# The first layer's attention mask, two levels earlier in POOL's chain of table instructions

## The chip, the cores and the metric

The kernel runs on one core of a Trainium2 chip. The metric is the device time of one execution in microseconds (us). Before the change three runs took 1725.45, 1729.42 and 1731.07 us; the median is 1729.42 us. The engines are called as in the profile: PE (TensorE, matmuls), DVE (VectorE), ACT (ScalarE), POOL (GpSimd) and SP (SyncE, which issues the weight transfers).

## The reference

Two layers of a transformer-like trunk over 256 tokens of width 1024. Each layer mixes tokens by three branches, and then has a feed-forward part: dense in the first layer, eight experts with the two best per token in the second. Two of the branches matter here.

```
# stick-breaking attention, 8 heads of 64, query blocks of 128
z = q @ k.T * scale
valid = key_pos < q_pos
log_stay = where(valid, log_sigmoid(-z), 0)
tail = reverse_cumsum(log_stay) - log_stay
w = where(valid, exp(log_sigmoid(z) + tail), 0)
out = w @ v
# S5 state space branch, 16 groups of 64 states
s_t = (mag * (cos(angle) + i sin(angle))) * s_{t-1} + b_t     # complex
y = c_re . s_re - c_im . s_im
# merged = g0 * (attention @ w_a) + g1 * (ssm @ w_b) + g2 * (conv @ w_c)
```

## The kernel before

Activations are kept transposed (features on partitions, 256 tokens along the row), weights come as units of 1 MB through a ring of seven slots. Every weight unit is split into a high and a low part: ACT copies the high part (L1010), DVE subtracts to get the low part (L1245, 2048 elements per partition, the longest instruction that DVE has), and PE makes three products with them (L627). Each engine runs a program of its own, in order, and the engines meet only at semaphores. The order of the mixer's steps is one list for all engines, `STEPS`: q, k, v, then `z` 0 (scores of the first four heads), `bbT`, u, `softplus` 0, h, b, c, `tail` 0, `gC` 0, `bu` 0, `gC` 1, `attend` 0, `bu` 1, `gC` 2, `z` 1 and so on. Each engine leaves out the steps in which it has no part.

The attention of four heads goes: PE computes scores (`z`, L690 and L692), ACT takes Abs, Exp and Ln of them (L1080 to L1083), DVE adds the positive part (`softplus`, L1339, which signals `stay_ready`), POOL sets the invalid entries to zero (the first mask, two instructions at L1644, which signals `stay_masked`), PE adds the cumulative sums (`tail`, L698 and L700), ACT takes Exp (L1087, signals `w_ready`), POOL masks again (L1644, signals `w_masked`), PE multiplies by v (`attend`, L711 and L713).

The state space branch needs tables of cosine and sine of the angle times 0 to 255. POOL builds them in `ssm_parameters` by doubling: a level of n columns makes columns n to 2n from columns 0 to n in six instructions (L1698 to L1703) over 8 times n elements per partition, and five small ones (L1709 to L1713) square the power for the next level. There are eight levels, n from 1 to 128. After the last one `tables_ready` lets DVE rotate and scan the states (`bu`, L1366 to L1375), and POOL rotates them back (L1726 to L1731). `ssm_parameters(0)` stands ahead of all of POOL's steps of layer 0, so POOL would come to the first mask only behind the whole chain; for that reason the chain itself contains that one mask, between two levels (L1692 and L1693), and the step `softplus` 0 of layer 0 is left out of POOL's list. The second mask (step `tail` 0) stands in POOL's list behind the chain. In layer 1 the chain runs long before its tables are needed, and its masks stand in the list.

`WB` is 3: PE writes its products into three work banks in turn, and waits for the reader of the bank that it takes.

Of the kernel before, what the change touches and what calls it, by code (L numbers as in the profile page):

```python
# [7 lines left out]
def trunk_kernel(nc, x, gain_mix, w_in, lam_re, lam_im, log_dt, b_re, b_im, c_re, c_im, ssm_d, w_glu,  # L8
# [17 lines left out]
    L = x.shape[0]  # L26
# [30 lines left out]
    def rows(w):  # L57
        return w.rearrange("(k p) n -> p k n", p=P)
# [137 lines left out]
    with ctx:  # L196
# [1418 lines left out]
        def _(pool):  # L1615
            chain = [0]

            def link(ins):

                chain[0] += 1  # L1620
                ins.then_inc(pool_chain, 1)
                pool.wait_ge(pool_chain, chain[0])
# [16 lines left out]
            def mask(ready, number, masked):  # L1639

                pool.wait_ge(ready, number)
                for lo in (0, L):
                    blk = attn[:, :, lo:lo + P]
                    last = nc.gpsimd.affine_select(out=blk, in_=blk, compare_op=ALU.is_gt, fill=0.0,  # L1644
                                                   base=0, pattern=[[0, HB], [1, P]],
                                                   channel_multiplier=-1)
                    if lo == 0:
                        link(last)
                last.then_inc(masked, 1)

            def ssm_parameters(l):

                if l:
                    pool.wait_ge(states_used, l * SJ)
                    pool.wait_ge(work_done, Group((l - 1, "glu", 0)).done)
                js = slice(l * SJ, l * SJ + SJ)
                for c, (b_src, c_src) in enumerate(((b_re, c_re), (b_im, c_im))):
                    pool.dma_start(braw[:, c, :, :], b_src[l].rearrange("g p h -> (g p) h")
                                   .rearrange("(j s) h -> s j h", s=P)).then_inc(ssm_loaded, 16)
                    pool.dma_start(craw[:, c, :, :], c_src[l].rearrange("g p h -> (g p) h")  # L1660
                                   .rearrange("(j s) h -> s j h", s=P)).then_inc(ssm_loaded, 16)
                pool.dma_start(wglu[:, :, :], rows(w_glu[l])).then_inc(glu_loaded, 16)
                link(nc.gpsimd.memset(bbp[:, :, :], 0.0))
                link(nc.gpsimd.memset(cblk[:, :, :, :], 0.0))
                pool.wait_ge(ssm_loaded, 64 * (l + 1))
                pool.wait_ge(f_ready, 1)
                fr = f_re[:, js].unsqueeze(2).to_broadcast([P, SJ, GH])
                fi = f_im[:, js].unsqueeze(2).to_broadcast([P, SJ, GH])
                m = [rtmp[:, q, 0:SJ * GH].rearrange("p (j h) -> p j h", h=GH) for q in range(4)]
                link(tt(m[0], braw[:, 0, :, :], fr, ALU.mult))  # L1670
                link(tt(m[1], braw[:, 1, :, :], fi, ALU.mult))
                link(tt(m[2], braw[:, 1, :, :], fr, ALU.mult))
                link(tt(m[3], braw[:, 0, :, :], fi, ALU.mult))
                for par in range(2):
                    r = slice(par * P // 2, par * P // 2 + P // 2)
                    hs = slice(par * GH, par * GH + GH)
                    for c, op in ((0, ALU.subtract), (1, ALU.add)):
                        dst = bbp[r, c, :].rearrange("p (j h) -> p j h", h=2 * GH)[:, :, hs]
                        link(tt(dst, m[2 * c][r], m[2 * c + 1][r], op))
                    link(ts(cblk[r, 0, :, hs], craw[r, 0, :, :], 1.0, None, ALU.mult))  # L1680
                    link(ts(cblk[r, 1, :, hs], craw[r, 1, :, :], -1.0, None, ALU.mult))
                nc.gpsimd.memset(cosT[:, :, 0:1], 1.0).then_inc(bbp_ready, 1)

                pc, ps, p2, p3, p4 = [power[:, q, :] for q in range(5)]
                link(nc.gpsimd.memset(sinT[:, :, 0:1], 0.0))
                link(nc.gpsimd.tensor_copy(pc, cos1[:, js]))
                nc.gpsimd.tensor_copy(ps, sin1[:, js]).then_inc(c_ready, 1)
                pool.wait_ge(c_ready, l + 1)
                pool.wait_ge(bbp_ready, l + 1)
                n = 1  # L1690
                while n < L:
                    if l == 0 and 2 * n == L:  # L1692
                        mask(stay_ready, 1, stay_masked)  # L1693
                    old, new = slice(0, n), slice(n, 2 * n)
                    bc = pc.unsqueeze(2).to_broadcast([P, SJ, n])
                    bs = ps.unsqueeze(2).to_broadcast([P, SJ, n])
                    tmp = rtmp[:, :, :].rearrange("p t n -> p (t n)")[:, 0:SJ * n].rearrange("p (j n) -> p j n", n=n)
                    tt(cosT[:, :, new], cosT[:, :, old], bc, ALU.mult)  # L1698
                    link(tt(tmp, sinT[:, :, old], bs, ALU.mult))
                    tt(sinT[:, :, new], sinT[:, :, old], bc, ALU.mult)  # L1700
                    link(tt(cosT[:, :, new], cosT[:, :, new], tmp, ALU.subtract))
                    link(tt(tmp, cosT[:, :, old], bs, ALU.mult))
                    last = tt(sinT[:, :, new], sinT[:, :, new], tmp, ALU.add)  # L1703
                    n *= 2
                    if n == L:
                        last.then_inc(tables_ready, 1)
                        break
                    link(last)
                    link(tt(p2, pc, pc, ALU.mult))  # L1709
                    link(tt(p3, ps, ps, ALU.mult))  # L1710
                    link(tt(p4, pc, ps, ALU.mult))
                    link(tt(pc, p2, p3, ALU.subtract))
                    link(tt(ps, p4, p4, ALU.add))  # L1713

            for l in range(DEPTH):
                ssm_parameters(l)
                for kind, t in STEPS:
                    if kind == "softplus":
                        if (l, t) != (0, 0):
                            mask(stay_ready, 2 * l + t + 1, stay_masked)  # L1720
                    elif kind == "tail":
                        mask(w_ready, 2 * l + t + 1, w_masked)
                    elif kind == "bu":
                        pool.wait_ge(scanned, 2 * (l * SJ + t + 1))
                        s_re, s_im = sring[:, t % 4, 0, :], sring[:, t % 4, 1, :]
                        tt(rtmp[:, 0, :], s_re, cosT[:, t, :], ALU.mult)  # L1726
                        tt(rtmp[:, 1, :], s_im, sinT[:, t, :], ALU.mult)
                        tt(rtmp[:, 2, :], s_re, sinT[:, t, :], ALU.mult)
                        link(tt(rtmp[:, 3, :], s_im, cosT[:, t, :], ALU.mult))
                        link(tt(s_re, rtmp[:, 0, :], rtmp[:, 1, :], ALU.subtract))  # L1730
                        tt(s_im, rtmp[:, 2, :], rtmp[:, 3, :], ALU.add).then_inc(states_ready, 1)  # L1731
                        pool.wait_ge(states_ready, l * SJ + t + 1)
# [45 lines left out]
```

## Time and profile before

| | |
|---|---|
| median of three runs | 1729.42 us (1725.45 to 1731.07) |
| span of the profiled execution | 1727.6 us |
| what lies around the span, median less span | 1.8 us |
| PE busy | 1655.4 us, 96% |
| POOL busy | 252.5 us, 15% |
| DVE busy | 552.4 us, 32% |
| share of PE in the chain that ended last | 88% |
| share of POOL in it | 4% |

The profiled execution has no time of its own beside its span; the span stands 1.8 us below the median and within the three runs. "Busy" says how long an engine had an instruction in it. The chain that ended last follows the execution back from its last instruction, at each step to what released it, so its shares say which engine's speed the end hung on. The granted clock (PEclk) is a share of 2.4 GHz: 1.00 is 2.4 GHz, 0.50 is 1.2 GHz.

### The profile page before, as it was taken

To read this page: it belongs to the slowest core of one execution; us is meant where nothing else is said; L and a number is where in the kernel's file an instruction comes from. 1 tells how busy PE (TensorE), PEld (TensorE's weight loads), DVE (VectorE), ACT (ScalarE), POOL (GpSimd) and SP (SyncE) were. 2 spreads that over 40 slices of the span, in tenths; PEclk is the share of its full clock that TensorE was granted. 3 is DMA by queue.
4 is the path that set the end of the run, shared out by engine and by line. 5 is a ranking of instruction groups with operands and counts; after the bars stand their busy time and mean duration, and the time that the engine had idled before them with its cause. 6 is when DMAs were issued, how large, how long until landed. Compare 5 with 4: busy or idle time off the path is not lost.

```text
span 1727.6 us, 32135 instructions
## 1 busy us (share of the span) xinstructions
PE 1655.4 (96%) x14514; PEld 1004.5 (58%) x14514; DVE 552.4 (32%) x836; ACT 410.2 (24%) x524; POOL 252.5 (15%) x338
## 2 busy tenths in 40 slices
PE   7889989999989999899999999999999999999996
PEld 6868989999989879853332333433333323334333
DVE  6557567444454675431010011110010100111102
ACT  5442344444454523310010010100010100101002
POOL 3877278000000461000000000000000000000000
PEclk9989999999999999989999999999999999999998
DMA  9702574555545324569989999989999989999980
GB/s 279 247 25 74 153 225 148 195 179 187 179 139 172 122 74 149 218 270 358 399 324 362 397 362 383 360 341 388 391 357 398 349 336 400 358 384 377 351 332 25
DMA packets 192649, 465.12 MB, mean 269 GB/s; under 512 B 9600, under 2 KB 91520, under 8 KB 192512
## 3 DMA queue, kind: packets, MB, share of 16 engines
q1 hardware_dynamic: 189600, 461.40, 72.3%
q8 instruction: 115, 1.88, 0.4%
q0 software_dynamic: 416, 1.05, 0.3%
q10 hardware_dynamic: 2496, 0.61, 0.2%
q14 instruction: 22, 0.18, 0.0%
HBM read 461.98 MB, written 1.05 MB: 268 GB/s over the span
## 4 chain that ended last, share of the span: by engine, by line
PE 88%; POOL 4%; DVE 4%; ACT 2%; issue 1%; ACTq 0%; DVEq 0%; POOLq 0%
PE work L627 28%; PE acc L892 23%; PE acc L920 17%; PE ssm_y L892 11%; PE acc L627 5%; PE work L903 1%; PE ssm_y L737 1%; PE work L728 1%; DVE arena L1532 1%; PE work L641 1%; POOL arena L1700 1%; DVE arena L1263 1%; PE acc L698 0%; DVE parts L1245 0%; POOL arena L1703 0%
## 5 line engine op out<-in xcount | busy, mean ns | idle before, releaser
L627 PE MATMUL work<-xs,parts 128*128 128x256 f32 x3648 | 463.4, 287 | 16.8 <-DVE xs L1252 13.6
L627 PEld LDWEIGHTS work<-xs,parts 128*128 128x128 f32 x3648 | 450.1, 194 | 28.1 <-issue 25.0
L892 PE MATMUL acc<-ring,arena 128*32 128x512 f32 (+1 forms) x4096 | 435.2, 543 | 0.7 <-issue 0.7
L920 PE MATMUL acc<-ring,arena 128*32 128x512 f32 x2688 | 294.4, 592 | 1.4 <-ACT arena L1176 1.4
L1245 DVE TENSOR_TENSOR parts<-ring,parts 128x2048 fp32r<-128x2048 f32 x94 | 222.8, 2375 | 177.6 <-ACT parts L1010 177.5
L892 PEld LDWEIGHTS acc<-ring,arena 128*32 128x32 f32 x4096 | 131.0, 110 | 247.8 <-issue 227.2
L892 PE MATMUL ssm_y<-ring,arena 128*32 128x512 f32 (+1 forms) x2048 | 239.3, 539 | 0.0
L1010 ACT ACTIVATE parts<-ring 128x2048 fp32r<-128x2048 f32 x94 | 179.1, 1910 | 122.6 <-PE work L627 69.5
L920 PEld LDWEIGHTS acc<-ring,arena 128*32 128x32 f32 x2688 | 85.8, 110 | 196.6 <-issue 192.9
L1541 DVE TENSOR_TENSOR arena<-arena,acc 64x256 f32<-64x256 f32 (+1 forms) x32 | 12.5, 390 | 561.2 <-ACT arena L1171 561.2
L1171 ACT ACTIVATE arena<-acc 64x512 f32<-64x512 f32 (+1 forms) x96 | 51.6, 538 | 556.6 <-PE ssm_y L892 555.0
L892 PEld LDWEIGHTS ssm_y<-ring,arena 128*32 128x32 f32 x2048 | 66.5, 110 | 126.3 <-issue 115.3
L627 PE MATMUL acc<-hs,parts 128*128 128x256 f32 x672 | 82.8, 283 | 0.0
L627 PEld LDWEIGHTS acc<-hs,parts 128*128 128x128 f32 x672 | 81.6, 192 | 0.0
L1548 DVE COPY arena<-work 128x256 f32<-128x256 f32 (+1 forms) x32 | 12.4, 389 | 200.7 <-PE work L903 200.7
L1176 ACT ACTIVATE arena<-work 128x512 f32<-128x512 f32 (+1 forms) x32 | 17.4, 544 | 247.7 <-PE work L903 247.7
L1644 POOL TENSOR_SCALAR_AFFINE_SELECT arena<-arena 128x512 f32<-128x512 f32 x16 | 14.8, 924 | 282.8 <-DVE arena L1339 271.5
L1102 ACT ACTIVATE sig<-work 128x256 f32<-128x256 f32 x48 | 18.4, 384 | 136.7 <-PE work L627 136.7
L903 PEld LDWEIGHTS work<-ident,arena 128*128 128x128 f32 x168 | 18.3, 144 | 32.7 <-issue 23.9
L1389 DVE TENSOR_TENSOR arena<-sig,work 128x256 f32<-128x256 f32 x48 | 19.9, 415 | 53.8 <-ACT sig L1102 53.8
L903 PE MATMUL work<-ident,arena 128*128 128x128 f32 x168 | 28.2, 294 | 6.8 <-DVE arena L1532 4.4
L1726 POOL TENSOR_TENSOR arena<-arena 128x256 f32<-128x256 f32 x16 | 27.1, 1693 | 40.1 <-DVE arena L1375 40.1
(244 smaller groups left out, 1098.2 us busy)
## 6 DMA issues: line engine op xcount, KB each, us to landing
ring<-in_moe_w_gate SPq DMA_DIRECT2D x112, 1024.0 KB, 7.2
ring<-in_moe_w_up SPq DMA_DIRECT2D x112, 1024.0 KB, 9.4
ring<-in_moe_w_down SPq DMA_DIRECT2D x112, 1024.0 KB, 8.7
ring<-in_w_in SPq DMA_DIRECT2D x44, 1024.0 KB, 6.7
ring<-in_dense_w_gate SPq DMA_DIRECT2D x14, 1024.0 KB, 5.0
ring<-in_dense_w_up SPq DMA_DIRECT2D x14, 1024.0 KB, 5.0
ring<-in_dense_w_down SPq DMA_DIRECT2D x14, 1024.0 KB, 4.9
ring<-in_w_out SPq DMA_DIRECT2D x8, 1024.0 KB, 12.0
```

What stands on the lines that cost most here:

```text
L627: last = nc.tensor.matmul(out_ap, a, b, start=start and n == 0, stop=stop and n == len(pairs) - 1, skip_group_check=shared)
L641: last = nc.tensor.matmul(bank[:, 0:L], neg_ones[:, :], xnT[:, k, :], start=k == 0, stop=k == KT - 1)
L892: last = nc.tensor.matmul(region(x, ns), xe[:, k, c:c + GRP], w[:, kk, half * ns:half * ns + ns], start=k == 0, stop=k == KT - 1)
L903: last = nc.tensor.transpose(bank[:, f * P:f * P + P], erow[:, tile, f * P:f * P + P], ident[:, :])
L920: last = nc.tensor.matmul(acc[GRP * q:GRP * q + GRP, b, :], eh[:, kt % tiles, c:c + GRP], w[:, kk, half * OUT_COLS:half * OUT_COLS + OUT_C ...
L1010: nc.scalar.activation(parts[:, s % PARTS, 0, :], ring[:, n % RING, :], ACT.Copy)\
L1102: nc.scalar.activation(sig[:, n % 2, :], bank[:, 0:L], ACT.Sigmoid).then_inc(sig_ready, 1)
L1171: nc.scalar.activation(dst, src, ACT.Silu).then_inc(silu_set, 1)
L1176: nc.scalar.activation(eh[:, 0:tiles, P // 2:2 * SLOTS], bank[:, 0:tiles * P].rearrange("p (f n) -> p f n", n=P), ACT.Copy)\
L1245: tt(parts[:, s % PARTS, 1, :], ring[:, n % RING, :], parts[:, s % PARTS, 0, :].bitcast(F32), ALU.subtract).then_inc(lo_ready, 1)
L1389: tt(dst, sig[:, n % 2, :], bank[:, L:2 * L], ALU.mult).then_inc(gate_used, 1)
L1726: tt(rtmp[:, 0, :], s_re, cosT[:, t, :], ALU.mult)
```

## The change

The test that places the first layer's first mask in the chain of levels is changed from the last level (n = 128) to the one of 32 columns. Nothing else is changed.

```diff
--- before.py
+++ after.py
@@ -1689,7 +1689,7 @@
                 pool.wait_ge(bbp_ready, l + 1)
                 n = 1
                 while n < L:
-                    if l == 0 and 2 * n == L:
+                    if l == 0 and 8 * n == L:
                         mask(stay_ready, 1, stay_masked)
                     old, new = slice(0, n), slice(n, 2 * n)
                     bc = pc.unsqueeze(2).to_broadcast([P, SJ, n])
```

Of the instruction order only POOL's differs; PE, DVE, ACT and SP have the same rows in the same order. The first place is POOL ahead of the level of 32 columns (8x32 is 256 elements; L1712 and L1713 belong to the level ahead of it):

```order
 L1712 TENSOR_TENSOR power<-power 128x8
 L1713 TENSOR_TENSOR power<-power 128x8
+L1644 AFFINE_SELECT arena<-arena 128x4x128 x2
 L1698 TENSOR_TENSOR arena<-arena,power 128x8x32
 L1699 TENSOR_TENSOR arena<-arena,power 128x256
```

The mask's two instructions are added here, with their wait for `stay_ready`. The second place is POOL ahead of the level of 128 columns:

```order
 L1712 TENSOR_TENSOR power<-power 128x8
 L1713 TENSOR_TENSOR power<-power 128x8
-L1644 AFFINE_SELECT arena<-arena 128x4x128 x2
 L1698 TENSOR_TENSOR arena<-arena,power 128x8x128
 L1699 TENSOR_TENSOR arena<-arena,power 128x1024
```

They are taken out here. Behind the last level POOL's order is the same before and after: the rows are the end of the last level, the second mask, and the first rotation of states.

```order
L1701 TENSOR_TENSOR arena<-arena 128x8x128
L1702 TENSOR_TENSOR arena<-arena,power 128x1024
L1703 TENSOR_TENSOR arena<-arena 128x8x128
L1644 AFFINE_SELECT arena<-arena 128x4x128 x2
L1726 TENSOR_TENSOR arena<-arena 128x256
```

PE's order, the same before and after, has behind the tail step (L698, L700) two tiles of gate C with the state input between them, and then the attend step (L711, L713):

```order
L698 MATMUL acc<-arena,neg_incl 128x384
L700 MATMUL acc<-arena,neg_ones 128x128
L627 MATMUL work<-xs,parts 128x256 x24
L627 MATMUL work<-arena,br_slot 128x256 x2
L728 MATMUL work<-arena,bbT 128x256 x2
L627 MATMUL work<-xs,parts 128x256 x24
L627 MATMUL work<-arena,br_slot 128x256 x2
L711 MATMUL acc<-arena 64x256
```

Nothing moved on PE: the first mask releases L698 and the second one L711.

## Rows read from the trace of the kernel before

**Rows 1.** The page's head: span of the profiled execution.

```profile
span 1727.6 us, 32135 instructions
```

**Rows 2.** PE's waits, whole span: us in total, times, longest.

```profile
PE acc L698 <- POOL arena L1644: 13.4, 3, 10.6
```

**Rows 3.** PE in order of time: start, us, instruction, count, idle before.

```profile
58.73 23.27 PE L627 MATMUL work<-xs,parts 128*128 128x256 f32 x192
92.55 1.65 PE L698 MATMUL acc<-arena,neg_incl 128*128 128x384 f32 x2 [10.55 <-POOL arena L1644]
...
98.84 3.11 PE L627 MATMUL work<-xs,parts 128*128 128x256 f32 x24
...
106.78 1.03 PE L627 MATMUL work<-arena,br_slot 128*128 128x256 f32 x4
108.31 0.66 PE L711 MATMUL acc<-arena 128*64 128x256 f32 x4 [0.50 <-POOL arena L1644]
...
114.80 0.71 PE L690 MATMUL acc<-arena 64*128 64x256 f32 x4
```

**Rows 4.** POOL in order of time, 70 to 108 us.

```profile
70.44 0.62 POOL L1698 TENSOR_TENSOR arena<-arena,power 128x256 f32<-128x256 f32 x1
...
71.71 2.54 POOL L1700 TENSOR_TENSOR arena<-arena,power 128x256 f32<-128x256 f32 x1
74.22 2.78 POOL L1701 TENSOR_TENSOR arena<-arena 128x256 f32<-128x256 f32 x1
77.08 0.62 POOL L1702 TENSOR_TENSOR arena<-arena,power 128x256 f32<-128x256 f32 x1
77.78 0.73 POOL L1703 TENSOR_TENSOR arena<-arena 128x256 f32<-128x256 f32 x1
...
81.97 1.04 POOL L1698 TENSOR_TENSOR arena<-arena,power 128x512 f32<-128x512 f32 x1
...
91.15 1.34 POOL L1644 TENSOR_SCALAR_AFFINE_SELECT arena<-arena 128x512 f32<-128x512 f32 x2
92.46 1.90 POOL L1698 TENSOR_TENSOR arena<-arena,power 128x1024 f32<-128x1024 f32 x1
...
98.14 2.39 POOL L1701 TENSOR_TENSOR arena<-arena 128x1024 f32<-128x1024 f32 x1
...
102.59 4.37 POOL L1703 TENSOR_TENSOR arena<-arena 128x1024 f32<-128x1024 f32 x1
106.91 1.34 POOL L1644 TENSOR_SCALAR_AFFINE_SELECT arena<-arena 128x512 f32<-128x512 f32 x2
```

**Rows 5.** DVE in order of time, 69 to 105 us.

```profile
69.70 1.74 DVE L1339 SCALAR_TENSOR_TENSOR arena<-acc,arena 128x1536 f32<-128x1536 f32 x1
71.36 5.04 DVE L1245 TENSOR_TENSOR parts<-ring,parts 128x2048 fp32r<-128x2048 f32 x2
...
89.49 0.69 DVE L1357 TENSOR_TENSOR arena<-arena 128x512 f32<-128x512 f32 x1
102.41 2.29 DVE L1245 TENSOR_TENSOR parts<-ring,parts 128x2048 fp32r<-128x2048 f32 x1 [12.23 <-ACT parts L1010]
```

**Rows 6.** POOL in order of time, the second layer's first mask.

```profile
562.23 5.26 POOL L1644 TENSOR_SCALAR_AFFINE_SELECT arena<-arena 128x512 f32<-128x512 f32 x2 [263.43 <-DVE arena L1339]
```

**Rows 7.** Windows: stretch, length, busy (count) by engine, PEclk, DMA share, GB/s.

```profile
84.50:85.00 0.50, 0.00 (x0) 0.00 (x0) 0.50 (x1) 0.00 (x0) 0.50 (x1) 0.62 1.08 383
...
92.50:98.00 5.50, 5.45 (x13) 3.63 (x14) 0.00 (x0) 0.00 (x0) 5.42 (x3) 0.50 0.00 0
98.00:98.50 0.50, 0.50 (x3) 0.29 (x2) 0.00 (x0) 0.00 (x0) 0.50 (x2) 0.73 0.00 0
...
226.00:228.40 2.40, 0.20 (x2) 0.08 (x1) 1.63 (x4) 2.21 (x8) 2.08 (x5) 1.00 1.10 348
```

**Rows 8.** PE in order of time, the second layer's tail step.

```profile
572.84 0.81 PE L698 MATMUL acc<-arena,neg_incl 128*128 128x384 f32 x2
...
576.23 0.36 PE L627 MATMUL work<-xs,parts 128*128 128x256 f32 x1
```

## The prediction

> **What bounds the kernel now.** I read the page's busy table first: PE is busy for 96% of a span of 1727.6 us [rows 1], so a change that removes no PE work can only change PE's waits or its clock. Next the table of PE's waits: PE waits for POOL's mask ahead of the tail matmuls three times, 13.4 us in all, and one wait of 10.6 us is most of it [rows 2]. That is the wait at which this change aims. Then PE and POOL in order of time around it. PE is done with its projections at 82.00 (58.73 + 23.27), sits idle for 10.55 us and starts the tail at 92.55, when POOL's first mask is through [rows 3, 4]. It then works without a gap to 107.81, and its attend step starts at 108.31 after only 0.50 us of waiting for POOL's second mask [rows 3].
>
> The reader should see in POOL's rows that POOL never rests from 70.44 to the end of the second mask at 108.25 (106.91 + 1.34), and that this mask comes behind the last level of the tables (102.59 + 4.37 = 106.96) [rows 4]. So the attend step is released by the length of POOL's whole chain, not by the place of the first mask in it. The 10.55 us idle of PE are real, but they are slack of a race that POOL loses a moment later: PE has 0.50 us to spare at 108.31. PE's order keeps attend in front of everything that follows, so PE can't run past it.
>
> **The change part by part.**
>
> *The early mask's wait.* At 70.44 POOL begins the level of 32 columns. In the changed order it first waits for DVE's softplus, which starts at 69.70 and ends at 71.44 [rows 4, 5]. POOL starts the mask about 0.06 us later, at 71.50, so 1.06 us of POOL's time are lost. Before, the result was 19.7 us old when the mask came, and nothing was waited for. Queued behind this wait are all of levels 32, 64 and 128, the second mask and the rotations: DVE waits for the tables, PE for the second mask.
>
> *The mask itself.* Two instructions leave 91.15 to 92.46 (1.31 us of pitch) and come in at 71.50. As far as they run alone they cost nothing net. But at 71.36 DVE starts two weight splits in a row, 5.04 us together, until 76.40 [rows 5]. POOL's instructions that fall on such a split are long: L1700 takes 2.54 and L1701 2.78 us there, and the same sizes on L1702 and L1703, a moment later, 0.62 and 0.73 us [rows 4]. That is 1.92 + 2.05 = 3.97 us of blocking. The second layer has just the new situation, the mask directly behind the softplus: its two instructions take 5.26 us there instead of 1.34 [rows 6, 4], 3.92 us of blocking. So the mask takes over the blocking from L1700 and L1701, one for the other: 3.92 - 3.97 = -0.05 us. The mask ends at 71.50 + 5.26 = 76.76, and nobody is late for it, since PE comes to the tail at 82.00.
>
> The Trainium skill, SBUF — State Buffer, section "SBUF: two separate sides", says of this that a DVE instruction with two SBUF inputs and a GpSimd instruction share one port pair, which the first to start holds to its end while the other fully blocks. By that rule the mask must be blocked as in the second layer; if instead it ran through in 1.34 us, the level behind it would meet the same two splits, and the sum would be nearly the same. The rows bear the rule out (2.54 us beside 0.62).
>
> *The three levels.* Their work is the same. Two further splits meet the chain: one shortly after the two above, which stays where it is, and the one that before ran from 102.41 and cost L1703 about 4.37 - 2.39 = 1.98 us [rows 4, 5]. It becomes early, because ACT's Exp of the tail is early, and falls at about 90 behind L1357, which ends at 90.18 [rows 5]; POOL is in the level of 64 columns then, and pays about the same 2 us there. What changes is only which instruction is hit, and whether it is in flight already (then DVE waits) or about to start. I take +0.4 us for this: a small power instruction made way for larger ones. Sum for POOL: 1.06 - 0.05 + 0.4 = +1.4 us. Bounds: +0.5 (one partial overlap falls better than before by half a us) and +3.0 (one more instruction of 2 us is hit, less 0.4). The tables are ready at 106.96 + 1.4 = 108.4, and attend starts at 108.31 + 1.4 = 109.7.
>
> *The tail on PE.* It starts at 82.0 instead of 92.55. In the second layer, where PE doesn't wait, the same matmuls take 576.23 - 572.84 = 3.39 us; here they take 98.84 - 92.55 = 6.29, since the granted clock, after it fell at about 84.6, stayed at 0.50 (1.2 GHz) until about 98.3 [rows 3, 7, 8]. In the changed kernel the tail runs at 2.4 GHz and ends at 85.4, the two gate tiles take their 8.97 us (98.84 to 107.81) [rows 3], and between them PE waits for the convolution, whose last instruction ends at 90.18 [rows 5], at most 1.7 us. PE stands at attend at 94.4 to 96.1. It idles there until 109.7, so 13.6 to 15.3 us. The idle is not gone: it has moved behind the two tiles, and grown.
>
> *The clock behind it.* The 10.55 us of idle were followed by 5.7 us at 1.2 GHz (92.55 to about 98.3, from the window with a mean of 0.73) [rows 3, 7]. That cost 6.29 - 3.39 = 2.9 us, hidden before, because PE waited for POOL at the end in any case. An idle of 2.2 us left the clock at 1.00 (226.00 to 228.40) [rows 7]; one of 13.6 us is beyond the 10.55 that dropped it. So the low clock now falls on attend, `bu` 1 and the start of `gC` 2, which stand on the path: PE then goes to `z` 1 (114.80), whose scores start the chain through ACT, DVE and POOL to the second tail. 5.7 us at half speed do 2.85 us of work, so `z` 1 comes 2.9 us later again. I take 2.7, as the clock's rise was not always at the same distance from the restart. Bounds: 0 (it does not fall) and 6.5 us, if it stays low for all that lies from 108.31 to 114.80 [rows 3]. No later wait absorbs it: what follows hangs on `z` 1 or on PE itself.
>
> The Trainium skill, TensorE: Matmul & The Clock Gate, section "Part 1: The HAM clock gate", says that what is slow after an idle is a stretch of time and not a number of matmuls, and that its end varies from run to run. By that the price would be the same for the small attend matmuls as for the tail, and differ by some tenths of a us between executions.
>
> *Sum.* +1.4 (POOL) + 2.7 (clock) = +4.1 us. Against its own span 1727.6 becomes 1731.7; with the 1.8 us around it, which is the distance to the median, 1729.4 becomes 1733.5 us.
>
> **The rivals.**
>
> A: the wait at 92.55 was on the path and its removal counts. PE would save up to 10.55 us, and the kernel take 1729.4 - 10.5 = 1718.9. For it: it is the longest wait of PE on another engine [rows 2]. Against it: attend waits for the second mask behind the tables. It decides if POOL's second mask could come before about 97; the rows of POOL leave no way for that. This is the case on the other side.
>
> B: POOL's delay alone, with the clock back quickly or hardly fallen: +1.4, at most +0.5 more, 1731. For it: the fall and rise are not fixed to the restart. Against it: the idle is longer than the one that cost 2.9.
>
> C: the clock stays low longer, since attend and `bu` use less of the array than the tail does, or a second 2 us block hits POOL: +1.4 + 4.5 or +3.0 + 2.9, so about +6 and up to +9: 1735.4 to 1738.4.
>
> D: the change does nothing, since PE was waiting for POOL's chain before and after and POOL's length hardly moves: 0 to +0.5, 1729.6. For it: PE's order is the same. Against it: the softplus ends 1.00 us after POOL gets there, and the hidden clock cost loses its cover.
>
> **How the numbers follow.** The forecast (+2.5 to +5.5) gets 0.55, A 0.05, B 0.15, C 0.18, D 0.07. About 0.3%, 5.2 us, is what a measurement of this kernel can tell from no change; the runs before lie 5.6 us apart. The forecast lies below this, so "within 0.3%" holds most of the forecast, B and D: 0.66. Slower by more is C and the upper edge of the forecast with the scatter of a median: 0.29. Faster is A: 0.05. The likeliest case alone spans 1731.9 to 1734.9. The range takes in B and D and most of C, and the scatter of the runs: 1728.5 to 1738.
>
> **What would show it.** In the changed profile: a POOL wait of about 1 us for L1339 at 70.4, then L1644 with some 5.3 us; PE's wait at L698 gone, and one of 12 to 15 us at L711; tables ready and L711 about 1.4 us later than now; a granted clock of 0.50 around 110 to 115 and of 1.00 at 82 to 86; from `z` 1 on everything about 4 us later, with no further difference. Wrong would be: L711 starting before 108 (then the chain on POOL is shorter than I think), a clock of 1.00 at 110 (B), or a distance between the traces that changes after 130.

## The result, and the profile after

The changed kernel takes 1733.53 us (median of 20 runs), the kernel before 1729.49 us in the same comparison (20 runs). The ratio is 1.0022, with a 95% interval of 1.0015 to 1.0029: slower by 4.0 us, within 2.6 to 5.0. The forecast was 1733.5. The span of the profiled execution is 1729.9 us against 1727.6 [rows 1].

The waits of PE over the whole span come first (us in total, times, longest). The wait of 10.6 us ahead of the tail [rows 2] is gone, and one of 15.3 us ahead of attend stands in its place:

```profile
PE acc L711 <- POOL arena L1644: 15.3, 1, 15.3
...
PE acc L698 <- POOL arena L1644: 2.8, 2, 1.4
```

PE in order of time around it, to hold against [rows 3]:

```profile
57.37 23.28 PE L627 MATMUL work<-xs,parts 128*128 128x256 f32 x192
80.48 0.81 PE L698 MATMUL acc<-arena,neg_incl 128*128 128x384 f32 x2
...
83.88 3.11 PE L627 MATMUL work<-xs,parts 128*128 128x256 f32 x24
...
91.81 1.03 PE L627 MATMUL work<-arena,br_slot 128*128 128x256 f32 x4
108.09 1.13 PE L711 MATMUL acc<-arena 128*64 128x256 f32 x4 [15.25 <-POOL arena L1644]
...
115.85 0.71 PE L690 MATMUL acc<-arena 64*128 64x256 f32 x4
...
128.84 0.91 PE L698 MATMUL acc<-arena,neg_incl 128*128 128x384 f32 x2 [1.42 <-POOL arena L1644]
```

The tail starts at 80.48, without a wait, directly behind the projections, and takes 3.4 us instead of 6.29. PE is through both gate tiles at 92.84 and then idles for 15.25 us, since attend starts at 108.09 where it started at 108.31 before. The attend matmuls take 1.13 us where they took 0.66. POOL in order of time, against [rows 4]:

```profile
69.71 0.20 POOL L1713 TENSOR_TENSOR power<-power 128x8 f32<-128x8 f32 x1
70.11 5.20 POOL L1644 TENSOR_SCALAR_AFFINE_SELECT arena<-arena 128x512 f32<-128x512 f32 x2 [0.20 <-DVE arena L1339]
75.28 0.61 POOL L1698 TENSOR_TENSOR arena<-arena,power 128x256 f32<-128x256 f32 x1
...
83.33 1.29 POOL L1698 TENSOR_TENSOR arena<-arena,power 128x512 f32<-128x512 f32 x1
...
88.55 2.98 POOL L1702 TENSOR_TENSOR arena<-arena,power 128x512 f32<-128x512 f32 x1
...
104.41 2.34 POOL L1703 TENSOR_TENSOR arena<-arena 128x1024 f32<-128x1024 f32 x1
106.70 1.34 POOL L1644 TENSOR_SCALAR_AFFINE_SELECT arena<-arena 128x512 f32<-128x512 f32 x2
```

The mask's two instructions take 5.20 us, the level of 32 columns begins at 75.28 with no softplus left to wait for, one instruction of the level of 64 takes 2.98 us, and none of the level of 128 is longer than 2.34, where L1703 took 4.37. DVE has the other half of the story, against [rows 5]:

```profile
68.23 1.74 DVE L1339 SCALAR_TENSOR_TENSOR arena<-acc,arena 128x1536 f32<-128x1536 f32 x1
69.89 4.92 DVE L1245 TENSOR_TENSOR parts<-ring,parts 128x2048 fp32r<-128x2048 f32 x2
...
84.93 1.42 DVE L1357 TENSOR_TENSOR arena<-arena 128x512 f32<-128x512 f32 x1
87.44 3.18 DVE L1245 TENSOR_TENSOR parts<-ring,parts 128x2048 fp32r<-128x2048 f32 x1 [1.10 <-ACT parts L1010]
```

The two weight splits start at 69.89, 0.22 us ahead of the mask, and the split that ran at 102.41 is now at 87.44. The convolution's last instruction starts at 84.93 instead of 89.49. Last, windows over PE's clock (the column behind POOL's busy time is the granted clock), of the changed kernel:

```profile
96.00:98.00 2.00, 0.00 (x0) 0.00 (x0) 0.00 (x0) 0.00 (x0) 2.00 (x2) 0.78 0.00 0
109.50:112.00 2.50, 2.50 (x15) 1.54 (x12) 2.00 (x4) 0.00 (x0) 1.42 (x3) 0.74 0.00 0
112.00:113.00 1.00, 1.00 (x9) 1.00 (x10) 0.97 (x3) 0.00 (x0) 1.00 (x2) 1.00 0.00 0
228.00:232.00 4.00, 2.68 (x13) 2.41 (x14) 3.93 (x10) 3.98 (x9) 3.50 (x7) 0.78 1.10 368
232.00:236.00 4.00, 4.00 (x29) 4.00 (x28) 3.29 (x3) 1.58 (x2) 3.72 (x4) 0.79 0.37 145
```

and of the kernel before, for the stretches that are new here:

```profile
109.50:112.00 2.50, 2.50 (x19) 1.94 (x16) 2.50 (x6) 0.52 (x1) 1.21 (x2) 1.00 0.00 0
...
228.00:232.00 4.00, 3.65 (x24) 3.19 (x25) 4.00 (x9) 3.98 (x6) 3.50 (x6) 1.00 1.07 380
232.00:236.00 4.00, 4.00 (x35) 4.00 (x35) 2.59 (x3) 1.36 (x3) 3.56 (x10) 1.00 0.33 109
```

The clock falls at about 97, during the idle, and is at 1.2 GHz from the start of attend to about 110.8. And it is low once more between 228 and 236, where it stayed up before. Both kernels idle for 2.1 to 2.2 us there, ahead of the output projection. The changed kernel starts the projection at 229.32, and the clock falls behind that start and not in the idle:

```profile
229.00:230.00 1.00, 0.68 (x4) 0.59 (x5) 1.00 (x3) 1.00 (x5) 0.92 (x2) 1.00 1.10 347
230.00:231.00 1.00, 1.00 (x5) 0.82 (x6) 1.00 (x3) 1.00 (x2) 0.82 (x3) 0.62 1.13 371
```

From 0.62 in the second window and 0.79 in the one from 232 to 236 it is low from about 230.2 to 233.7. In the second profile of the changed kernel the projection starts at 231.21 and the clock falls at about 232.2.

Each kernel was profiled twice. The execution's own start scatters by about 1 us (POOL begins the parameter work at 35.14 and 34.34 us before, 34.26 and 35.45 after), so the stretches are compared and not the absolute times. All are differences of starts and ends in the timelines:

| stretch | before | before, again | after | after, again | difference of means |
|---|---|---|---|---|---|
| POOL: parameter work to the second mask's end | 73.11 | 73.60 | 73.78 | 74.23 | +0.65 |
| second mask's end to the start of z 1 on PE | 6.55 | 6.53 | 7.81 | 7.91 | +1.32 |
| z 1 to the output projection | 113.55 | 113.48 | 113.47 | 113.62 | +0.03 |
| output projection to the sum of squares behind it | 25.53 | 25.53 | 26.61 | 26.61 | +1.08 |
| from there to the second layer's | 250.25 | 249.24 | 250.24 | 250.25 | +0.50 |

The first four sum to +3.1 us, inside the interval of 2.6 to 5.0. The fifth is scatter: it is 1 us shorter in one of the profiles of before, and the same in the three others. The remaining 1 us or so of the 4.0 is in none of these stretches. The wait for the softplus was 0.20 us in the first profile and 1.22 in the second, whose rows (POOL) are

```profile
71.77 5.20 POOL L1644 TENSOR_SCALAR_AFFINE_SELECT arena<-arena 128x512 f32<-128x512 f32 x2 [1.22 <-DVE arena L1339]
...
108.34 1.34 POOL L1644 TENSOR_SCALAR_AFFINE_SELECT arena<-arena 128x512 f32<-128x512 f32 x2
```

### The profile page after: what moved, and what is told of

Same layout as the page of the kernel before. It is cut to its first block, busy times and chain, and to the rows that moved or that the text cites. A ratio compares the mean times of both kernels' runs of the same rounds, so it can differ in the third digit from the quotient of the medians.

```text
span 1729.9 us, 32135 instructions
## 1 busy us (share of the span) xinstructions
PE 1654.6 (96%) x14514; PEld 1005.4 (58%) x14514; DVE 550.8 (32%) x836; ACT 409.7 (24%) x524; POOL 253.4 (15%) x338
## 4 chain that ended last, share of the span: by engine, by line
PE 89%; DVE 4%; ACT 3%; POOL 2%; issue 1%; ACTq 0%; DVEq 0%; POOLq 0%
PE work L627 29%; PE acc L892 23%; PE acc L920 17%; PE ssm_y L892 11%; PE acc L627 5%; PE work L903 1%; PE ssm_y L737 1%; PE work L728 1%; DVE arena L1532 1%; DVE parts L1245 1%; ACT parts L1010 1%; POOL arena L1644 1%; DVE arena L1263 0%; PE acc L698 0%; POOL arena L1702 0%
## 5 line engine op out<-in xcount | busy, mean ns | idle before, releaser
L1644 POOL TENSOR_SCALAR_AFFINE_SELECT arena<-arena 128x512 f32<-128x512 f32 x16 | 18.6, 1163 | 283.9 <-DVE arena L1339 272.7
```

## The experiments

Each was timed in the same comparison with the kernel before. "Under" and "over" are from the medians there.

**The first mask ahead of the level of 64 columns.**

```diff
-                    if l == 0 and 8 * n == L:
+                    if l == 0 and 4 * n == L:
```

> The first mask one level later than in the changed kernel, ahead of the level of 64 columns. Theory (POOL's chain releases attend, and PE restarts there at 1.2 GHz): POOL comes to the mask about 82, long after the softplus (71.4), so the wait for DVE goes, and two weight splits fall on L1700 and L1701 again as before. The mask ends about 83.3, 1 to 3 us after PE is there; the idle ahead of attend stays at 11 to 14 us and its clock cost too. Time: before + 0 (POOL) + 1.3 to 2.9 (clock) = +1.5 to +3.5 us, a little under the changed kernel's +4.0. Rival (the softplus wait and the blocked mask make the whole difference): as before, +0 to +0.5. Rival (early tail as such is a gain): below before.

Measured: 1732.96 against 1729.72 us, ratio 1.0021 (1.0012 to 1.0030). The mask waits for nothing and is blocked by nothing (82.34, 1.34 us), PE waits 2.46 us for it and 10.77 us at attend. POOL's stretch to the second mask is 73.70 us, z 1 starts 7.99 us behind it, and the output projection takes 26.69 us. So the softplus wait and the blocked mask are not the main cost: without either the kernel is still 3.2 us over before, and by the medians 0.8 of the 4.0 us are theirs (the two intervals, 2.1 to 5.2 and 2.6 to 5.0 us, overlap). It is enough that the mask comes early and lets PE run ahead.

**PE kept busy ahead of attend, in the changed kernel.**

```diff
                     elif kind == "attend":
+                        if (l, t) == (0, 0):
+                            for _ in range(110):
+                                nc.tensor.matmul(ssm_y[:, 0, :], x_parts[0][:, 0, 0:P], x_parts[1][:, 0, :],
+                                                 start=True, stop=True, skip_group_check=True)
```

> The changed kernel with 110 filler matmuls (128x256, 0.12 us each, 13.2 us in all) on PE ahead of the first layer's attend 0, into a PSUM bank that is not yet in use; PE works instead of idling. Theory: the granted clock stays at 1.00, attend and what follows run at 2.4 GHz, the clock term of 1.3 to 2.9 us goes and POOL's 1.1 to 1.4 us stay: before + 1.0 to +1.5 us, 2.5 to 3 us under the changed kernel. Rival (the clock costs nothing there, all of +4.0 is POOL's): +4.0, as the changed kernel. Rival (fillers reach beyond the mask): later than the changed kernel.

Measured: 1731.01 against 1729.72 us, ratio 1.0004 (0.9995 to 1.0013), 1.3 us over before by the medians, where the changed kernel was 4.0 over. Work without use made the kernel faster. The windows show a clock of 1.00 in the idle and in attend:

```profile
96.00:106.00 10.00, 10.00 (x85) 10.00 (x85) 0.00 (x0) 0.06 (x1) 9.84 (x5) 1.00 0.00 0
108.00:110.00 2.00, 0.16 (x2) 0.16 (x4) 1.40 (x4) 0.00 (x0) 1.72 (x3) 1.00 0.00 0
110.00:112.00 2.00, 2.00 (x19) 1.59 (x18) 1.90 (x5) 0.00 (x0) 0.00 (x0) 1.00 0.04 8
```

z 1 starts 6.54 us behind the second mask, as before, so the 1.3 us of that stretch are the clock's. The rest of the gain of some 2.7 us is not from there. A later stretch, the second layer's output projection, took 24.78 us instead of 26.28 in this profile, as the clock stayed up there too; but so it did in four other profiles, one of them with fillers as well and three without, so it is not shown that the fillers did it. POOL's stretch to the second mask was 75.00 us here, 1.0 more than the changed kernel's mean.

**PE kept busy ahead of the tail, in the kernel before.** The same loop with 75 matmuls ahead of `tail`.

> The kernel before with 75 such filler matmuls (9 us) ahead of its tail 0, in the idle of 10.5 us. Theory: the tail runs at 2.4 GHz and ends 2.9 us earlier, but PE then only waits 3.4 us instead of 0.5 for the second mask: +-0.3 us against before. Rival (low clock behind the idle costs the kernel before its 2.9 us in full): -2.5 to -2.9.

Measured: 1733.42 against 1729.72 us, ratio 1.0020 (1.0011 to 1.0029). Neither the theory as I had put it nor the rival. The order of POOL is that of before, its second mask ends at 108.08 against 108.25, and yet the kernel is as slow as the changed one. PE's rows say why:

```profile
103.91 1.03 PE L627 MATMUL work<-arena,br_slot 128*128 128x256 f32 x4
108.14 1.13 PE L715 MATMUL acc<-arena 128*64 128x256 f32 x4 [3.20 <-POOL arena L1648]
109.05 0.65 PE L717 MATMUL acc<-arena 128*64 128x128 f32 x4
...
116.07 0.71 PE L690 MATMUL acc<-arena 64*128 64x256 f32 x4
```

The tail runs fast, PE is through the gate tiles at 104.94 and idles for 3.20 us, and attend starts at the low clock (L713, here L717, takes 0.65 us, before 0.39). The granted clock there is

```profile
108.00:109.00 1.00, 0.86 (x4) 0.54 (x6) 0.93 (x3) 0.00 (x0) 0.09 (x1) 0.50 0.00 0
```

The idle was short, and I had put its price at zero. z 1 is 7.99 us behind the mask's end. So the changed kernel's time can be had without moving the mask: what matters is that PE comes early to attend.

**PE kept busy in both places, in the kernel before.** 75 matmuls ahead of the tail and 27 ahead of attend.

> The kernel before with fillers in both idles of PE: 75 ahead of tail 0 and 27 (3.2 us) ahead of attend 0. It tells apart why fillers ahead of the tail alone cost 3.5 us. Theory: they moved PE's idle (3.2 us) to attend, and the granted clock fell there; POOL's chain and the release of attend were as before (108.08 against 108.25). With PE busy there too, the time from the second mask's end to z 1 is 6.5 us instead of 8.0 and the kernel takes the time of before, -0.5 to +1.0 us. Rival (the fillers themselves disturb, by SBUF or PSUM traffic or by what the earlier tail triggers on ACT and DVE): +3 to +4 us again.

Measured: 1730.49 against 1730.58 us, ratio 1.0003 (0.9994 to 1.0013). The 3.7 us of the run ahead are gone, which excludes the fillers' own traffic as their cause. But the profile warns against reading the zero as a clean one: the fillers end 1.6 us behind the mask (attend at 110.13, mask's end at 108.49), attend to z 1 then takes 6.48 us, at full clock, and about as much comes back where the clock stayed up later, at the second layer's output projection (24.78 us instead of 26.28). What of the 3.7 us is attend's clock and what is such scatter, one profile of each kernel can't tell.

**POOL's chain shortened, in the changed kernel.** This kernel leaves out the second product of the sine table's upper half, but for one column.

```diff
-                    link(tt(tmp, cosT[:, :, old], bs, ALU.mult))
-                    last = tt(sinT[:, :, new], sinT[:, :, new], tmp, ALU.add)
+                    if l == 0 and 2 * n == L:
+                        last = tt(sinT[:, :, 0:1], sinT[:, :, 0:1], tmp[:, :, 0:1], ALU.add)
+                    else:
+                        link(tt(tmp, cosT[:, :, old], bs, ALU.mult))
+                        last = tt(sinT[:, :, new], sinT[:, :, new], tmp, ALU.add)
```

> The changed kernel with the last two instructions of the first layer's last table level left out but for one column (L1702 and L1703 at 128 columns, 1.90 + 2.34 us; the sine table's upper half is then incomplete). Theory: the end of POOL's chain releases attend, so attend comes 4.2 us less about 0.3 earlier, and the kernel ends 3.7 to 4.2 us earlier than the changed kernel, near the time before; PE's wait at attend falls from 15.3 to about 11.3 us and the clock term stays. Rival (PE waits for something else, or the delay is absorbed later): the same time as the changed kernel.

Measured: 1729.82 against 1729.72 us, ratio 0.9999 (0.9990 to 1.0008): 0.1 us over before where the changed kernel was 4.0 over, so 3.9 us less. The wait fell from 15.25 to 11.15 us, and everything behind it came earlier:

```profile
104.82 1.13 PE L711 MATMUL acc<-arena 128*64 128x256 f32 x4 [11.15 <-POOL arena L1644]
...
112.75 0.71 PE L690 MATMUL acc<-arena 64*128 64x256 f32 x4
```

POOL's stretch is 69.67 us, 4.3 less than the changed kernel's mean, and no later wait gave it back. This shows that the end of POOL's chain releases attend, and that a microsecond there is about one of the kernel.

**Both masks inside the chain.**

```diff
+                    if l == 0 and 2 * n == L:
+                        mask(w_ready, 1, w_masked)
...
                     elif kind == "tail":
-                        mask(w_ready, 2 * l + t + 1, w_masked)
+                        if (l, t) != (0, 0):
+                            mask(w_ready, 2 * l + t + 1, w_masked)
```

> The changed kernel with the first layer's second mask (behind the Exp of tail 0) moved into the chain too, ahead of the level of 128 columns; PE's order unchanged. Theory (attend is released by the end of the chain only because its mask stands behind it): attend starts at about 96 instead of 108, and PE then waits at gate C tile 2, whose bank is released by DVE's first read behind the tables, at about 109.5, 1 us later than attend was released before, but with attend and bu 1 (2.6 us) already done; the idle is 12 us and the clock falls. Time: changed kernel - 2.6 + 1.3 = -1 to -2 us, so before + 2 to +3. Rival (a gain as large as the idle): 8 us or more under before. Rival (another engine holds attend): no change against the changed kernel.

Measured: 1731.47 against 1730.58 us, ratio 1.0007 (0.9998 to 1.0016), 0.9 us over before, a little better than expected; the interval takes in no change. PE's rows:

```profile
95.80 0.66 PE L711 MATMUL acc<-arena 128*64 128x256 f32 x4 [2.89 <-POOL arena L1644]
...
109.70 4.85 PE L627 MATMUL work<-xs,parts 128*128 128x256 f32 x24 [9.66 <-DVE arena L1369]
```

Attend comes 12 us earlier, and the idle moves to the next place that hangs on the tables: the bank that DVE reads first behind them (L1369). An idle of 9.66 us stays.

**The state input later in PE's order, both layers.** With both masks in the chain:

```diff
-    BU_AFTER = [0, 1, 3, 4, 6, 7, 9, 10]
-    YS_AFTER = [3, 4, 6, 7, 9, 10, 12, 13]
+    BU_AFTER = [4, 5, 6, 7, 8, 9, 10, 11]
+    YS_AFTER = [7, 8, 9, 10, 11, 12, 13, 14]
...
-        if t == 1:
+        if t == 2:
             STEPS.append(("attend", 0))
-        if t == 2:
+        if t == 3:
             STEPS.append(("z", 1))
-        if t == 3:
+        if t == 4:
             STEPS.append(("softplus", 1))
-        if t == 4:
+        if t == 5:
             STEPS.append(("tail", 1))
```

> Both masks in the chain as in the run with two masks, and in addition the state input steps (bu 0 to 7, which need the tables) three to four gate tiles later, ys after them, attend 0 behind gate C tile 2 and z 1 behind tile 3, softplus 1 behind 4, tail 1 behind 5. Theory: the idle of PE can be filled only by work that doesn't need POOL's chain; PE then goes through tail 0, five gate tiles, attend 0 and z 1 without a wait up to about 108, when the tables are ready. Of the 15 us idle some 10 to 14 go, and the clock stays up: 8 to 14 us under before (1716 to 1722). Rival (the state space chain of bu, scan, rotation and ys on DVE and POOL, now squeezed between tiles 4 and 14, becomes the bound and gives the gain back at gelu and glu): 0 to 5 us under before. Rival (the wait for the tables only moves): no gain.

Measured: 1731.13 against 1730.58 us, ratio 1.0005 (0.9996 to 1.0014). The forecast of 8 to 14 us less failed; by the time alone the rivals (0 to 5 us less, or no gain) were nearer. Two stretches of PE's rows tell where it went. The first layer:

```profile
98.20 0.66 PE L711 MATMUL acc<-arena 128*64 128x256 f32 x4 [2.61 <-POOL arena L1644]
...
118.80 1.65 PE L698 MATMUL acc<-arena,neg_incl 128*128 128x384 f32 x2 [4.57 <-POOL arena L1644]
...
221.77 13.42 PE L627 MATMUL work<-xs,parts 128*128 128x256 f32 x94 [2.12 <-DVE xs L1252]
```

Attend waits 2.61 us instead of 15.25, z 1 starts at 103.63, 11 us earlier, and tail 1 then waits 4.57 us for its mask and restarts at the low clock (1.65 us for what takes 0.91 before). The output projection starts at 221.77, 6.6 us earlier than in the profile of before. The second layer:

```profile
602.71 1.65 PE L698 MATMUL acc<-arena,neg_incl 128*128 128x384 f32 x2 [4.57 <-POOL arena L1644]
...
705.99 14.26 PE L627 MATMUL work<-xs,parts 128*128 128x256 f32 x117 [2.04 <-DVE xs L1252]
```

It has the same wait at tail 1, which was 1.42 us before, and takes 207.50 us from its first sum of squares to its output projection instead of 200.87: 6.6 us lost, all that the first layer won. PE has no other new wait in this stretch, none at `gelu` or `glu` either, where a rival had seen the bound: the wait at tail 1 is 3.2 us longer, and the tail step, at the low clock, takes 6.6 us where it took 3.7.

**The new order in the first layer alone.** `STEPS` becomes one list for each layer; the second layer's is the old one.

```diff
+        bu_after = [0, 1, 3, 4, 6, 7, 9, 10] if l else [4, 5, 6, 7, 8, 9, 10, 11]
+        ys_after = [3, 4, 6, 7, 9, 10, 12, 13] if l else [7, 8, 9, 10, 11, 12, 13, 14]
+        attend, z, softplus, tail = (1, 2, 3, 4) if l else (2, 3, 4, 5)
```

> The reordered kernel with its order in the first layer alone; the second layer keeps the order of before. In the reordered kernel's profile the first layer ends its gates 6.6 us earlier than before (221.8 against 228.4), and the second layer gives 6.6 us back, with a new wait of 4.6 us at tail 1 and 200.0 us instead of 193.4 from projection to projection. Theory (the gain of filling PE's idle is real, and the loss comes from the same order in a layer whose tables are ready long before): before - 4.5 to - 6 us, 1724.5 to 1726. Rival (a gain in layer 0 is lost later whatever layer 1 does): about before.

Measured: 1724.16 against 1729.89 us, ratio 0.9966 (0.9954 to 0.9978). This is the best version, 5.7 us under before, and by the two distances 9.8 under the changed kernel. The second layer is back at 201.01 us.

**Tail 1 one gate tile later.** `tail` of the first layer is 6 instead of 5.

> As the run with the new order in the first layer alone, with tail 1 one gate tile later (behind tile 6). Theory (its wait of 4.6 us for the second half's first mask, and the low clock behind it, 2.9 us, are idle that one tile of 4.1 us fills): 4 to 7 us less than that run, 8 to 12 us under before. Rival (attend 1, still behind tile 7, now waits for its mask, since Exp and mask of tail 1 take about 6 us and only tile 7 and bu 3 lie between): the wait comes back at attend 1, 0 to 3 us less than that run.

Measured: 1725.41 against 1729.89 us, ratio 0.9970 (0.9958 to 0.9982): 1.25 us over the run ahead of it, with intervals that overlap. The theory (4 to 7 us less) failed. The rival had the mechanism, a wait that comes back at attend 1, but not the size (0 to 3 us less). The wait of 4.58 us at tail 1 is gone, and three others take its place, at the state input (which waits for its bank's reader, a gate product that DVE does late), at the gate tile behind it, and at attend 1 (this file's lines stand 6 further down):

```profile
117.37 1.13 PE L734 MATMUL work<-arena,bbT 32*128 32x256 f32 x4 [1.50 <-DVE arena L1395]
120.36 5.32 PE L633 MATMUL work<-xs,parts 128*128 128x256 f32 x24 [1.87 <-DVE arena L1375]
...
136.70 0.66 PE L717 MATMUL acc<-arena 128*64 128x256 f32 x4 [1.69 <-POOL arena L1650]
```

**The first mask at 64 columns in the new order.** As the run ahead of it, with `4 * n == L`.

> As the run with tail 1 later, but the first mask ahead of the level of 64 columns. It asks what the place of the first mask is worth once PE has work behind the tail that doesn't hang on POOL's chain. Theory: the mask comes at about 83.7 as in the first run with that place, PE waits 2.5 us at tail 0 and restarts at a low clock; 2 to 4.5 us more than the run with the mask ahead of the level of 32. Rival (the place is worth nothing here either, since tail 1 and attend 1 set the pace): 0 to 0.5 us more.

Measured: 1726.34 against 1729.89 us, ratio 0.9977 (0.9966 to 0.9988), 0.9 us over the run with the mask at 32, with intervals that overlap. This lies between the rival's 0 to 0.5 us more and the theory's 2 to 4.5. PE does wait 2.46 us at tail 0. But POOL, which doesn't stop for the softplus and the splits, has its second mask through at 95.58 instead of 98.37, and attend starts at 98.00 against 98.42. So even where PE has other work, the place of the first mask is worth little here: what it gives PE at the tail it takes from POOL ahead of attend.

**The kernels before and after once more, for second profiles.**

> The kernel before once more, for a second profile. It tells how much of the difference between two profiles is scatter of one execution: in the profile of before PE's clock stayed at 1.00 through the idle of 2.2 us at 226, in the changed kernel's and in all four experiments it fell there and cost about 1.1 us. Theory (that fall comes and goes from run to run): z 1 starts 6.5 us after the second mask's end as before, and the stretch from the start of the output projection to the sum of squares takes 25.5 or 26.6 us, either is possible. Rival (the earlier tail changes something that lasts until 228): 25.5 us again.

The stretch was 25.53 us again, and z 1 started 6.53 us behind the mask.

> The changed kernel once more, for a second profile. Theory: its second mask ends within 1 us of that of before (106.7 + 1.3 = 108.0 in the profile of after, 107.9 to 108.3 in two of before), z 1 starts 7.8 to 9.4 us behind it instead of 6.5, as the granted clock is 0.50 at attend, and the clock falls in the idle of 2.1 us at about 228 again. Rival (the chain on POOL is the larger part): the second mask ends 1.4 us or more later than before.

Its second mask ended at 109.68, which is 1.6 us later than in the first, but the execution began its parameter work 1.2 us later. Against the first profile of before the mask ends 1.43 us later, which is the sign that the rival had named; from the start of the parameter work it is 0.9 us over the mean of before (74.23 against 73.36), and the clock's 1.3 us stay the larger part. It was 7.91 us to z 1, and 26.61 us for the output projection.

## Why the prediction was right

**The wait off the path.** Right. PE's longest wait of 10.55 us went, and the kernel did not get faster. The chain of POOL releases attend; PE's gate tiles ran ahead and PE waited 15.25 us (13.6 to 15.3 had been worked out). It is at the upper end because the two tiles ran without the wait for the convolution that had been allowed for, and PE was through them at 92.84 and not at 94.4 to 96.1; attend, for its part, started at 108.09 (109.73 in the second profile) where 109.7 had been forecast. The shortened chain showed it from the other side.

**POOL's term, +1.4 us.** Right in sign, too large: the two pairs of profiles give +0.65 us, with 0.5 us between the two of a pair. The softplus wait, taken as 1.06, was 0.20 and 1.22 us, since POOL and DVE come to that point 1 us apart from one execution to the next. The blocking of the mask, worked out as 3.92 us from the second layer, was 5.20 - 1.34 = 3.86. The Trainium skill, SBUF — State Buffer, "SBUF: two separate sides", has POOL and a DVE instruction with two SBUF inputs exclude each other for whole instructions; by that rule the trace agrees. The rows agree in both directions: where POOL was first, DVE's split grew from 2.29 to 3.18 us at 87.44. That the blocking would stay the same in sum held, and the +0.4 that I added for it was not needed.

**The clock at attend, +2.7 us.** The mechanism was right, the size was off. The clock was at 1.2 GHz at the restart in both profiles of the changed kernel, and z 1 came 1.32 us later for it. What failed is the step that carried the 5.7 us of low clock from the tail over to attend. In the first profile the clock was up again at 110.8, 2.7 us behind the restart. In the second it was 0.66 in the window from 112 to 113, so up at about 112.7, 3.0 us behind it. The Trainium skill, TensorE: Matmul & The Clock Gate, "Part 1: The HAM clock gate", says that the end of the slow stretch varies by 500 ns either way between runs. Two profiles of one kernel agree with that (2.7 and 3.0 us behind attend's restart, 5.7 and 5.3 us behind the tail's in the two of before). The distance between the two places is larger, and its cause is open.

**No later difference.** Wrong. I had written that from z 1 on nothing would change. From z 1 to the output projection nothing did (+0.03 us). There the clock fell 0.9 us behind the end of an idle of 2.1 us, at a place where it had stayed at 1.00 before, and the stretch took 1.08 us more. The prediction had named a distance between the traces that changes after 130 as a sign of being wrong, and this is one. I had read the 2.2 us of idle in the trace as too short for a fall; it is not. In both profiles of before the stretch is 25.53 us, in the other twelve 26.27 to 26.75. That speaks for the changes as its cause, but doesn't show it: it happens in kernels with quite different first layers, with and without fillers, and with the unmoved mask, and each profile is one execution. And such a fall does come and go with nothing changed ahead of it. The two kernels with 75 fillers ahead of the tail are alike up to there, and idle for 2.63 and 2.61 us behind the fillers; in the first the clock stayed at 1.00, in the second it fell at about 94.1, 1.3 us behind the tail's start. No run took the fall at 230 away by itself, so whether its 1.08 us belong to the change is open.

So it is luck, in errors of opposite sign, that the number met the measured one to a tenth of a us: 0.7 us too much for POOL and 1.4 too much for the clock at attend, against 1.1 for the fall that I had excluded and the 1 us or so by which the timed runs lie above the sum of the stretches. What held without compensation is the mechanism of the two terms and the sign; the two terms alone measured 2.0 us of the 4.1 forecast.

**The rivals.** A (the wait was on the path) is excluded by the result. B (POOL alone) by the clock of 0.50. C was the same mechanism at a size that did not come (its upper end, +9 us, is not the sum of the terms shown for it). D (nothing changes) lies outside the interval.

## What to carry to other kernels

A long wait in the table of waits is worth nothing if the same engine releases the next thing in the queue later still: follow the releaser's program to its next signal before you take the wait out. A removed wait doesn't vanish, it moves to the next place, and there it can be dearer, because a matmul engine that has waited can restart at half its clock; here the idle ahead of the tail was hidden, and the one ahead of attend was not. Fill such an idle with work that doesn't hang on the late engine, and only in the layer that has it: the same reordering won 6.6 us in the first layer and lost 6.6 in the second.

## What the runs showed of the hardware

The length of a short idle doesn't decide whether PE's clock falls. An idle of 3.20 us had PE restart at 1.2 GHz for the next 3 us, and one of 2.61 us was followed by a fall too, while 2.63 us at the same place, and 2.82 us ahead of attend in the run with 110 fillers, left it at 1.00. Idles of 2.12 to 2.43 us ahead of the output projection made the stretch behind them longer in twelve profiles, while idles of 2.12 and 2.20 us there left the clock at 1.00 in the two of before. And the fall need not lie in the idle: in eleven of those twelve it came 0.4 to 1.5 us after PE had restarted (0.9 us in the changed kernel), so a look at the clock at the restart alone misses it. With 2.7 to 3.0 us of low clock behind an idle of 15.25 us and 5.7 behind one of 10.55, the price does not grow with the idle. 110 matmuls without a use made a kernel faster, by 2.7 us as the medians stand, of which 1.3 are seen at attend, where they kept the clock up. And the same stretch of code, the second layer's output projection, took 26.3 us in nine profiles and 24.8 in five: a difference of 1.5 us that comes as a step. It may be part of why runs of the same kernel lie up to 8 us apart (1725.45 to 1733.45); no run shows that.
